# Prompt row sums of a PEER layer: half of them by two tokens per TensorE tile, half fetched by token and added by VectorE

## The reference, cut to what matters

```python
q = (x @ w_q).reshape(N, PEER_HEADS, 2, PK_DIM // 2)
s = jnp.einsum("nhcd,ckd->nhck", q, sub_keys)
...                                   # top 16 of the sums of two keys; gate = softmax
def one(args):
    xb, ib, gb = args
    act = jax.nn.gelu(jnp.einsum("thkd,td->thk", u_tab[ib], xb)) * gb
    return jnp.einsum("thk,thkd->td", act, v_tab[ib])
```

## Time and profile before

| | us |
|---|---|
| median of 3 runs (lowest, highest) | 2686.32 (2685.88, 2694.42) |
| the profiled execution | 2693.58 |
| its span | 2691.8 |
| TensorE busy in the span | 2619.8 (97%) |
| VectorE, ScalarE, GpSimd busy | 1659.5, 1033.8, 725.7 |
| DMA engines, mean over the span | 262 GB/s |

### The profile page before, as it was taken

One profiled execution on the slowest core, in us unless ns is written; L12 is line 12 of the kernel. 1 busy time (PEld: TensorE's weight loads), 2 busy tenths in 40 slices (PEclk: granted clock), 3 DMA queues, 4 the chain that ended last, 5 costly groups with the idle time before them and its releaser, 6 DMA issues. The chain is left out here.

```text
span 2691.8 us, 39775 instructions
## 1 busy us (share of the span) xinstructions
PE 2619.8 (97%) x15961; PEld 2322.0 (86%) x15961; DVE 1659.5 (62%) x3313; ACT 1033.8 (38%) x1556; POOL 725.7 (27%) x680
## 2 busy tenths in 40 slices
PE   7998999999999999999999889999999999999998
PEld 6997788999999997777779769999999999777775
DVE  3437697878444456555576568987844445655556
ACT  3434433345433333333352654334543333333333
POOL 1001020000011117777723003000001111777773
PEclk9998899999999999999999899999999999999999
DMA  9643496457699869999963123335669986999995
GB/s 306 212 149 135 148 312 209 149 194 280 254 359 322 309 217 390 391 383 382 385 249 109 65 96 111 129 137 196 276 257 359 321 310 218 389 390 391 391 386 204
DMA packets 233111, 704.67 MB, mean 262 GB/s; under 512 B 22113, under 2 KB 154593, under 8 KB 211169
## 3 DMA queue, kind: packets, MB, share of 16 engines
q1 hardware_dynamic: 172912, 516.86, 52.0%
q0 software_dynamic: 59200, 184.79, 18.6%
q10 hardware_dynamic: 816, 0.48, 0.1%
HBM read 598.12 MB, written 103.94 MB: 261 GB/s over the span
## 5 line engine op out<-in xcount | busy, mean ns | idle before, releaser
L1414 PE MATMUL hidden_ps<-h_hi,u_hi 128*128 128x384 f32 x2016 | 680.1, 337 | 3.0 <-issue 2.0
L1414 PE MATMUL hidden_ps<-h_hi,u_lo 128*128 128x384 f32 x2016 | 674.0, 334 | 0.0
L1414 PE MATMUL hidden_ps<-h_lo,u_hi 128*128 128x384 f32 x2016 | 674.0, 334 | 0.0
L2322 DVE TENSOR_TENSOR v_lo<-v_slot,v_hi 128x1024 fp32r<-128x1024 f32 x248 | 303.8, 1225 | 265.6 <-ACT v_hi L2186 265.6
L2186 ACT ACTIVATE v_hi<-v_slot 128x1024 fp32r<-128x1024 f32 x248 | 263.0, 1060 | 514.7 <-PE out_ps L2115 511.3
L2115 PE MATMUL out_ps<-v_hi,act_hi 128*128 128x512 f32 x992 | 389.6, 393 | 0.0
L2115 PE MATMUL out_ps<-v_lo,act_hi 128*128 128x512 f32 x992 | 386.3, 389 | 0.0
L2115 PE MATMUL out_ps<-v_hi,act_lo 128*128 128x512 f32 x992 | 385.9, 389 | 0.0
L1414 PEld LDWEIGHTS hidden_ps<-h_hi,u_hi 128*128 128x128 f32 x2016 | 378.6, 188 | 5.1 <-issue 5.1
L1414 PEld LDWEIGHTS hidden_ps<-h_lo,u_hi 128*128 128x128 f32 x2016 | 378.7, 188 | 0.0
L1414 PEld LDWEIGHTS hidden_ps<-h_hi,u_lo 128*128 128x128 f32 x2016 | 378.4, 188 | 0.0
(11 more groups left out here) (510 smaller groups left out, 4018.5 us busy)
## 6 DMA issues: line engine op xcount, KB each, us to landing
u_slot<-in_peer_u SPq DMA_DIRECT2D x64, 2048.0 KB, 8.7
v_slot<-in_peer_v SPq DMA_DIRECT2D x64, 2048.0 KB, 10.0
hidden<-hidden_ring SPq DMA_DIRECT2D x64, 768.0 KB, 5.6
spread_gates<-spread SPq DMA_DIRECT2D x16, 2048.0 KB, 7.2
hidden_in<-hidden SPq DMA_DIRECT2D x64, 512.0 KB, 14.9
ada_w_ring<-in_ada_w SPq DMA_DIRECT2D x48, 512.0 KB, 6.0
even_w_ring<-in_even_w SPq DMA_DIRECT2D x16, 1024.0 KB, 7.0
ada_w_ring<-in_ada_w SPq DMA_DIRECT2D x16, 1024.0 KB, 6.3
```

The lines of the kernel that those rows point to most:

```text
L1414: mm = pe.matmul(PH_[:, b, 0:T], u[:, b, k * P:(k + 1) * P], x[:, k, :], start=(k == 0 and part == 0), stop=(k == KB - 1 and part == 2))
L2322: dve.tensor_tensor(lo, V[o // JC % 2][:, o % JC, :], hi.bitcast(F32), ALU.subtract).then_inc(vl, 1)
```

## The change

The picks of the prompt are divided by heads. Picks of heads 0 to 3 (64 of each token) are handled as before, but two tokens share a tile: partitions 0 to 63 hold the picks of one token, partitions 64 to 127 those of another, 16 tokens further. A group of four tiles now covers eight tokens; there are 16 groups (`QUADS`), one in each burst, and the ring for them has 7 slots.

Picks of heads 4 to 7 are "own rows": own row j is the fetch of pick 64 + j of all 128 tokens, so that partition t holds a row of token t. VectorE multiplies it by the token's value and adds it to `SUM0` (`add_own_row`), at steps S-1, S, S+2 and S+3 around the burst after product S (`OWN_AFTER`). The other four slots of the old ring hold own rows. At the end `SUM0` is added to the prompt's sums in PSUM.

`picks(i)` now has eight fetches. ScalarE, not VectorE, makes the high part of the activations (`act_high`), ahead of v_hi in its order. The gelu values are kept by tile (`HG`, `HD`, `HV`), so a load of the latent activations is one run of 4 KB per partition instead of four of 1 KB, and the gating multiplies are issued per tile. In `peer_front`, VectorE copies the picks of heads 0 to 3 twice side by side ahead of the transpose, ScalarE takes them apart in six copies and adds one for heads 4 to 7, and the index arithmetic has three more instructions.

```diff
+                PAIRED = M.at("paired_picks", M.picks, [P, 3, 2, HALF_PICKS])
...
-                        act.activation(HG[:, m % 2, j, :], PH_[:, n % 2, 0:T], ACT.Gelu_apprx_tanh).then_inc(g_done, 1)
+                        act.activation(HG[:, m % 2, :, j, :], PH_[:, n % 2, 0:T].rearrange("p (t k) -> p t k", t=TT), ACT.Gelu_apprx_tanh).then_inc(g_done, 1)
...
+                            for s in range(2):
+                                r = slice(HALF_PICKS * s, HALF_PICKS * (s + 1))
+                                for kind in range(3):
+                                    act.activation(PICK0[r, kind, 0:HALF_PICKS].rearrange("p (g i) -> p g i", g=4),
+                                                   PT[r, kind * P:(kind + 1) * P].rearrange("p (g h i) -> p g h i", g=4, h=2)[:, :, s, :], ACT.Copy)
+                            act.activation(PICK0[:, :, HALF_PICKS:P], GS[:, 0, :, HALF_PICKS:P], ACT.Copy).then_inc(pk_taken, 1)
...
-                RING, FREE = len(SLOT_AT), 2
+                RING, FREE = 7, 2
                 ROWS = [M.at(f"row_slot{n}", o, [P, D]) for n, o in enumerate(SLOT_AT)]
+                OWN = ROWS[RING:]
+                SUM0 = M.at("row_sum", 4096, [P, D])
...
-                QUADS = P // 4
-                SET = 2
-                SET_AFTER = [15 + 7 * i for i in range(16)]
+                QUADS = HALF_PICKS // 4
+                SET_AFTER = [15 + 7 * i for i in range(QUADS)]
+                OWN_AFTER = {SET_AFTER[j // 4] + (-1, 0, 2, 3)[j % 4]: j for j in range(HALF_PICKS)}
...
-                        sp.dma_start(HV[:, c % 2], HD[:, c, :, P:T]).then_inc(hg_in[c % 2], 16)
+                        sp.dma_start(HV[:, c % 2], HD[:, c, 1:TT]).then_inc(hg_in[c % 2], 16)
...
-                    def row_sums(s):
-                        groups = range(SET * s, SET * s + SET)
-                        pe.wait_ge(acts_made, SET * s + SET)
-                        for i in groups:
-                            for j in range(4 * i, 4 * i + 4):
...
+                    def row_sums(i):
+                        pe.wait_ge(acts_made, i + 1)
+                        for j in range(4 * i, 4 * i + 4):
+                            pe.wait_ge(slot_in[j % RING], 16 * (j // RING + 1))
...
+                    def act_high(o):
+                        c, j = divmod(o, JC)
+                        if j == 0:
+                            act.wait_ge(hg_in[c % 2], 16 * (c // 2 + 1))
+                        if 3 <= o < LATE:
+                            act.wait_ge(o_done, o - 2)
+                        hi = AH[:, o % 3, :] if o < LATE else AHX[:, o - LATE, :]
+                        act.activation(hi.rearrange("p (t k) -> p t k", t=2), HV[:, c % 2, :, j, :], ACT.Copy).then_inc(ah_ready, 1)
...
                     for o in range(2, N_KEYS):
+                        act_high(o)
                         v_part(o)
...
+                    def own_row(j):
+                        n, at = j % len(OWN), HALF_PICKS + j
+                        if j >= len(OWN):
+                            pool.wait_ge(own_added, j - len(OWN) + 1)
+                        pool.indirect_dma_start(OWN[n], None, table,
+                                                bass.IndirectOffsetOnAxis(ap=IDXV[:, at:at + 1], axis=0)).then_inc(own_in[n], 16)
...
-                        for g in range(4):
-                            t = token(i, g)
-                            pool.indirect_dma_start(ACT0[:, t:t + 1], None, hidden,
+                        for at in [QUADS * g + i for g in range(4)] + [HALF_PICKS + 4 * i + g for g in range(4)]:
+                            pool.indirect_dma_start(ACT0[:, at:at + 1], None, hidden,
...
                     for j in range(FREE, RING):
                         row(j)
+                    for j in range(len(OWN)):
+                        own_row(j)
                     picks(2)
                     picks(3)
-                    at = RING
                     for i in range(QUADS):
-                        while at < min(P, RING + 4 * i + 4):
-                            row(at)
-                            at += 1
+                        for j in range(RING + 4 * i, min(HALF_PICKS, RING + 4 * i + 4)):
+                            row(j)
+                        for j in range(len(OWN) + 4 * i, min(HALF_PICKS, len(OWN) + 4 * i + 4)):
+                            own_row(j)
                         if i + 4 < QUADS:
                             picks(i + 4)
...
+                    def add_own_row(j):
+                        n, w = j % len(OWN), ACT0[:, HALF_PICKS + j:HALF_PICKS + j + 1]
+                        dve.wait_ge(acts_made, j // 4 + 1)
+                        dve.wait_ge(own_in[n], 16 * (j // len(OWN) + 1))
+                        if j == 0:
+                            dve.tensor_scalar(SUM0[:, :], OWN[n], w, None, ALU.mult).then_inc(own_added, 1)
+                        else:
+                            dve.wait_ge(own_added, j)
+                            dve.scalar_tensor_tensor(SUM0[:, :], OWN[n], w, SUM0[:, :], ALU.mult, ALU.add).then_inc(own_added, 1)
...
+                        if o in OWN_AFTER:
+                            add_own_row(OWN_AFTER[o])
...
+                                dve.wait_ge(own_added, HALF_PICKS)
+                                f = PO[:, 0, half, :]
+                                v.seq(dve.tensor_tensor(f, f, SUM0[:, half * CH:(half + 1) * CH], ALU.add))
```

More of the change, by code:

```diff
@@ L1610, in picks @@
                         for kind in range(3):
[L1611 removed]
+                            src = PAIRED[:, kind].rearrange("p a k -> p (a k)") if t == 0 else GS[:, t, kind, :]
+                            mm = pe.transpose(PT[:, kind * P:(kind + 1) * P], src, ident)
                         mm.then_inc(turned, 1)
@@ L1892, in row_numbers @@
                         v.wait()
-                        v.mark(dve.scalar_tensor_tensor(IDXG[:, :], first, float(T), iota, ALU.mult, ALU.add))
+                        for s in range(2):
+                            r = slice(HALF_PICKS * s, HALF_PICKS * (s + 1))
+                            groups = lambda x: x[r, 0:HALF_PICKS].rearrange("p (g i) -> p g i", g=4)
+                            v.mark(dve.scalar_tensor_tensor(groups(second), groups(first), float(T),
+                                                            iota[r].rearrange("p (g h i) -> p g h i", g=4, h=2)[:, :, s, :], ALU.mult, ALU.add))
+                        v.mark(dve.tensor_scalar(second[:, HALF_PICKS:P], first[:, HALF_PICKS:P], float(T), CST[:, C_IDX:C_IDX + 1],
+                                                 ALU.mult, ALU.add))
                         v.mark(dve.scalar_tensor_tensor(ACT0[:, :], IDIG[:, :], -31.75, ACT0[:, :], ALU.mult, ALU.add))
                         v.wait()
+                        v.mark(dve.scalar_tensor_tensor(IDXG[:, :], IDIG[:, :], float(P - T), second, ALU.mult, ALU.add))
                         v.seq(dve.tensor_scalar(IDXV[:, :], ACT0[:, :], 4.0, float(l * N_KEYS * N_KEYS), ALU.mult, ALU.add))
@@ L2019, in peer_experts @@
                 slot_in = [sem(st, f"row_in{n}") for n in range(RING)]
+                own_in = [sem(st, f"own_row_in{n}") for n in range(len(OWN))]
+                own_added, ah_ready = sem(st, "own_row_added"), sem(st, "act_hi_ready")
                 pick_in = [sem(st, f"picked_in{n}") for n in range(8)]
@@ L2315, in gate_early @@
                         dve.wait_ge(early_w[e % 2], 16 * (e // 2 + 1))
-                        a = each_key(HV[:, e % 2])
-                        dve.tensor_tensor(a, a, each_group(WE[:, e % 2]), ALU.mult).then_inc(early_gated, 1)
+                        for t in range(2):
+                            a = each_key(HV[:, e % 2, t])
+                            ins = dve.tensor_tensor(a, a, each_group(of_tile(WE[:, e % 2], t)), ALU.mult)
+                        ins.then_inc(early_gated, 1)
                     def v_part(o):
@@ L2362, in _ @@
                         if o + 2 in SET_AFTER:
-                            for i in range(SET):
-                                act_columns(SET * SET_AFTER.index(o + 2) + i)
+                            act_columns(SET_AFTER.index(o + 2))
+                        if o in OWN_AFTER:
+                            add_own_row(OWN_AFTER[o])
                     if out is None:
```

68 lines of the change are left out of this document (39 added, 29 removed).

## The result

The kernel became slower: 2805.3 us, the median of runs between 2799.5 and 2810.5, against 2687.4 us for the kernel before on the same chip. The ratio is 1.0425, with a 95% interval from 1.0406 to 1.0444. The direction was forecast; the size was not: 2697.5 us with a range up to 2722. The profiled execution has a span of 2808.4 us against 2691.8, so 116.6 us have to be found.

The account below looks back on a forecast made before the run. TensorE was taken to set the time, with GpSimd's serial fetches near their limit; -57.1 + 2 x 18.3 + 2 x 12.0 + 7.5 = +11.0 us on the 2686.32 us median gave 2697.5 us, range 2670 to 2722.

Parts of the forecast that it names:

- row sums: Second stage, bursts on TensorE: half the matmuls take 1.785 us a burst, 57.1 us saved in all.
- start of the stage: Second stage's start: own row 4, 46th fetch in GpSimd's order, stalls TensorE by the second burst, 18.3 us a layer.
- loop, 28 periods: Periods between bursts: own rows behind shared rows make each 21.9 us, not 21.05; 12 us a layer.
- ends of the layers: After the last burst: VectorE's remaining work and adding SUM0 cost 4.4 us in layer 0, 3.1 in layer 1; 7.5 together.
- stages ahead: Before the second stage: pick copies and added index operations cost nothing, at most 1.3 us a layer without cover.
- the third view: List of GpSimd's issues: 16 fetches with gaps cost it 21.4 of 22.84 us a period, so TensorE's gain isn't all kept.
- 11.8 + L: Least period in the second-stage loop, L being an own row's landing: 5.2 to 14.4 us, window medians averaging 9.25.
- GpSimd's 21.4 us as a floor: Second-stage loop: GpSimd's 16 serial fetches and their gaps keep a period at 21.4 us or more.
- The loads: V chunks and activations, second stage: same bytes in longer runs cost nothing, or 1 us in each of 16 chunk pairs.
- the sign that I had called wrong: Listed sign against the forecast, second stage: an activation (hidden_in) load landing after v_hi is wanted; no size given.
- the fetches queue up: Rival, second stage: period 22.6, start 22 us, half clock for one stretch a layer; +43 us, 2729 us; chance 0.07.
- GpSimd is blocked by VectorE: Rival, second-stage loop: each add lengthens an issue by 1.23 us, GpSimd's period 26.3 us; 123 us more; chance 0.02.

Follow-up runs that it names:

- reordered kernel: Changed kernel with two own rows issued ahead of the four shared rows and fewer picks ahead of the own rows at the stage's start: 2692.5 us, ratio 1.0009.
- layout alone: Kernel before with only gelu values kept by tile (activation loads in 4 KB runs) and ScalarE making the activations' high part: 2691.4 us, ratio 1.0013.

## Why the prediction was wrong, point by point

The terms of its sum against the trace, in us of both layers:

| term | forecast | measured | how measured |
|---|---|---|---|
| row sums | -57.1 | -57.1 taken as the base | bursts of 1.85 to 1.90 where nothing stalls; period 21.15 |
| start of the stage | 36.6 | 42.6 | second burst 86.1 and 85.9 after the stage's first product, 64.7 without a stall |
| loop, 28 periods | 24.0 | 123.4 | 25.14 and 25.77 against 21.05 |
| ends of the layers | 7.5 | 11.4 | last burst to the end: 40.7 against 36.1 - 1.8; layer 0, to the next stage: 896.1 against 892.8 - 1.8 |
| stages ahead | 0 | -3.6 | the first second-stage product at 986.9 against 990.5 |
| sum | 11.0 | 116.7 | span 2808.4 - 2691.8 = 116.6 |

- **What bounds the kernel, and the direction**: right. TensorE's gain was real (21.15 us periods in the reordered kernel) and was taken by GpSimd's order, as the third view said.
- **GpSimd at the start**: right in kind, 21.3 us a layer against 18.3. Own row 4 is the 46th fetch; it is issued 62.4 us after the first pick (forecast 63.6) and lands 10.7 us later, not 9.0. The reordered start takes the stall away whole.
- **The loop of the own rows**: the mechanism is right, and its size is the step that failed, by 99 of the 106 us that the sum is short: the period came at 25.5 us and not at 21.9. The formula was 11.8 + L with L = 9.25. Three parts of it were small. First and largest, L: in the twelve turns of layer 1 that the chain shows from the second burst on, the first own row of a group lands after 8.8 to 15.6 us, 12.1 on average, and the step chose "the mean over rows behind none to three of them", though the text said itself that the own row stands behind four. The shared rows ahead of it have a median of 9.1 us, and with two own rows in front of them the medians come together (10.5 for own rows, 10.9 for shared ones), so the place in the queue is one part; the V loads beside it are another, 3.5 us by the run that thinned them. Secondly, the issues: from the burst's start to the own row's issue it is 7.5 to 8.6 us, not 1.785 + 5.6 = 7.4; in the turns with 8.6 one of the four issues ahead takes 1.7 to 2.0 us, as the 1.99 above. Thirdly, the clock: many a product behind a wait takes 4 to 5.5 us in place of 2.75. Start and loop together lost 166 us, of which 118.8 are waits; the other 47 are mainly products at the lower clock, for TensorE was busy 2608.2 us where 2619.8 - 57.1 = 2562.7 were due, 45.5 more. I had kept 2.5 us a stall "for the upper end", for one stretch a layer; there were 28 waits in the two layers, 17 of them with a slow product behind.
- **GpSimd's 21.4 us as a floor**: too low as well. 16 issues took 22.8 us once the adds ran beside them. In the kernel after this is hidden under the loop, but for one turn of layer 1 (2624.33 to 2654.07), where the chain runs through GpSimd's issues of a whole group; the reordered kernel met it.
- **The loads**: right that they cost nothing in the loop (1.0013 with the layout alone, where TensorE waited 1.2 us in layer 1, for a shared row). Yet the sign that I had called wrong was there: in the kernel after ScalarE waited 64.6 us for activations.
- **The ends**: 11.4 against 7.5. VectorE's work behind the last burst sets them, as told, but not without a gap: in layer 1 it waited 1.83 us ahead of product 124's v_lo, because ScalarE awaited the last load of activations for 3.23 us (it landed at 2772.4, 4.7 us behind the start of the last burst). There the loads did cost, and I had put them at nothing.
- **The rivals**: "the fetches queue up" was the right one in kind, priced at a period of 22.6 and given 0.07; it came at 25.5. "GpSimd is blocked by VectorE" has the price that came nearest, 123 us more, but not by its mechanism: with the adds made thin the kernel still took 2750.7 us. By the rule of the Trainium skill (SBUF — State Buffer, SBUF: two separate sides) the loser of the shared port pair waits for the whole instruction; the page tells of starved fetches for VectorE's two-port modes, and has operations with two SBUF inputs, as the adds are, contend only with GpSimd operations that read SBUF. An add that blocked an issue whole would make it up to 1.28 us longer; the mean went up by 0.05 us, so the trace does not show such blocking. Yet where GpSimd is the bound the adds cost some 14 us in the loop (reordered kernel, thin adds), and I had given a smaller lengthening nothing.
- **The chances**: the range's upper end was worked out from the same L, so no bound of it stood for an own row behind four others. The rows had a price for that: the slowest landings, 14.4 us, which give 26.2 us by the formula.

What stays open: why GpSimd's issues grew longer by as much as its head start of some 6 us a layer, and how much of a late landing is the place in the queue alone, since the order changes the share of the DMA engines too.

## What to carry to other kernels

A fetch that is issued on an event and wanted before the next one closes a loop; its period is issue + landing + use, and the landing to put in is that of its own place in the queue, behind all that is issued ahead of it on the same event, with the slow rows of the trace as the bound. Issue first what is wanted first, and keep fetches that need no buffer (the picks here) out of the way of those that close the loop. And where an engine issues serially and has 6% of room, price each lengthening of an issue: here the same sums with the right order gave back all of the loss and none of the gain.

## What the runs showed of the hardware

- After an idle time of TensorE of 6.39 us the next product ran at a granted clock of 0.52 and took 5.36 us in place of 2.75, so the wait cost up to 2.6 us more than itself. The idle time alone did not decide it: after 2.33 us the clock was 0.61, after 3.13 us 1.00.
- Indirect fetches issued beside VectorE's 1.28 us adds took 1.126 us on average against 1.074 with the adds cut to 8 columns; the longest took 2.7 us against 2.0.
- Of eight row fetches of 512 KB that GpSimd issued in a row, the four in front had a median landing of 9.1 us and the four behind them 12.2; with the V loads beside them cut to a quarter, 6.1 and 8.7.
- The same bytes but for 2 KB of picks a period moved at 407 GB/s with a DMA share of 1.01 when GpSimd issued 12 fetches a period; in the kernel after, the share of 0.88 was a consequence of the waits and not a limit.
